# Three attentions whose transposes stand three pairs behind the scores

## The chip, the cores and the metric

The kernel runs on one core of one Trainium2 chip. The time is the device time of one execution in microseconds, and the median of several executions counts. Before the change it is 3695.54 us (three runs, 3688.07 to 3698.82).

## The reference

The input x has 512 tokens of 1024 features. Two blocks follow one another.

The first block has two layers. Each is a gated feed-forward part, a mixer, a second feed-forward part and a gated embedding, all with RMS norms before and after. The mixer joins a stick-breaking attention of 4 heads, a latent attention of 8 heads and a short gated convolution. The latent attention is a causal softmax attention whose queries and keys have 96 features (64 plain and 32 rotated), computed in four blocks of 128 queries:

```python
for start in range(0, S, Q_BLOCK):
    end = start + Q_BLOCK
    sc = (einsum(q_nope[:, start:end], k_nope[:, :end]) + einsum(q_rope[:, start:end], k_rope[:, :end])) * scale
    w = softmax(where(mask, sc, NEG_INF))
    outs.append(einsum(w, v[:, :end]))
```

The second block has two layers, too. The mixer of the first is the DSA attention: 12 query heads share 4 key and value heads, and each query attends to the 128 keys with the highest index score (min(256, 512 / 4)). The mixer of the second is the dilated attention: three patterns of 4 heads each, merged by their log sums. Beside each mixer stands a memory attention: 4 heads, a softmax over 256 memory tokens. Both layers end with a feed-forward part.

## The kernel before

**Layout.** Features lie on the 128 partitions and tokens along the free axis. Each weight is streamed by SyncE in pieces of 128x1024 floats and split by GpSimd into a high and a low part; TensorE multiplies high with high, low with high and high with low. During the attentions no piece is used.

**An attention.** `attend` exists three times, for TensorE (L780), ScalarE (L1142) and VectorE (L1460). The work is cut into rows, a row being one head and one block of 128 queries, and two rows make a pair. In the latent and the DSA attention row block b has b + 1 key blocks (for causality), so four pairs in a row have 1, 2, 3 and 4 key blocks; the latent attention has 16 pairs, the DSA attention 24. In the memory attentions all 8 pairs have 2 key blocks. Each pair goes through these steps:

- TensorE: scores of both rows, and the mask added by a matmul with the identity (L796, L802), into one of two pairs of PSUM banks (psA, psB). It first waits until the exponentials of pair j - 2 are done.
- VectorE: the row maxima, `peak` (L1481).
- ScalarE: the exponentials with their sums, `exponentials` (L1152). They are written to one of four places in the tile PR.
- VectorE: reciprocal and scaling, `normalize` (L1487, L1490).
- TensorE: transposes in groups of up to four 128x128 blocks, `turn_pair` (L813), into one of the two banks of psC. It waits for the normalization and, group by group, until the copy of the group two before has emptied the bank.
- ScalarE: the copy of each group to SBUF, `copy_turned` (L1163).
- TensorE: the products with the values, `weigh` (L827), into psD. It waits for that copy.
- After four pairs: ScalarE copies the output (L1174), and VectorE forms its low part (L1410).

**The order.** Each engine works its own queue in order, and that order is written out by a loop over j. `ahead_of` gives two numbers, `ahead` and `late`. `late` is the distance in pairs between the scores and the transposes. TensorE's loop is

```python
for j in range(len(pairs) + late + 1):
    if j < len(pairs):
        scores(j)
    if 0 <= j - late < len(pairs):
        turn_pair(j - late)
    if j - late - 1 >= 0:
        weigh(j - late - 1)
```

ScalarE's loop (L1166) has in iteration j the exponentials of pair j, then the copies of pair j - late, and when j - late is 4, 8, ... the output copy, which waits for all values up to pair j - late - 1. VectorE's loop (L1492) has in iteration j `peak(j)`, then `normalize(j - 1)`, and when j - late is 4, 8, ... the low part. In the DSA layer's memory attention VectorE also has up to 18 half rounds of the selection, two per iteration (L1466 to L1470), from the first iteration on.

Before the change (ahead, late) is (1, 1) for the dilated attention, which has wide scores and two score places, and (2, 2) for the others: the latent attention (once per layer of the first block), the DSA attention and both memory attentions.

Of the kernel before, what the change touches and what calls it, by code (L numbers as in the profile page):

```python
# [114 lines left out]
def program(nc, A, trips):  # L115
# [209 lines left out]

    def ahead_of(which):

        return (1, 1) if which == "dil" else (2, 2)

    def row_at(which):  # L330

# [193 lines left out]
    def _(pe):  # L525
# [254 lines left out]
        def attend(which):  # L780
            pairs = pairs_of(which)
            ahead, late = ahead_of(which)
            pe.wait_ge(rot_done, n.now(rot_done))
            pe.wait_ge(vt_done, n.now(vt_done))
# [205 lines left out]
    def _(act):  # L990
# [151 lines left out]
        def attend(which):  # L1142
            pairs = pairs_of(which)
            ahead, late = ahead_of(which)
            used_base, turns = n.now(pv_done), 0

# [100 lines left out]
    def _(dve):  # L1247
# [212 lines left out]
        def attend(which, half_rounds=0):  # L1460

            pairs = pairs_of(which)
            ahead, late = ahead_of(which)
            done = 0

# [374 lines left out]
```

## Time and profile before

| | |
|---|---|
| median of three runs | 3695.54 us |
| lowest, highest | 3688.07, 3698.82 us |
| the profiled execution | 3689.66 us |
| its span | 3688.4 us |
| TensorE busy | 3459.0 us (94%) |
| VectorE, ScalarE, GpSimd busy | 1802.9, 719.3, 2418.4 us |
| mean granted clock of TensorE | 0.958 |

The span is the time from the first to the last instruction of the program in the profile. "Granted clock" is the share of TensorE's full clock of 2.4 GHz that the chip gave; it is either 1.0 or 0.5. The chain that ended last is mostly TensorE's matmuls of the feed-forward parts and projections; the attentions are short stretches between them.

### The profile page before, as it was taken

The numbers are of one execution on the slowest core, as the hardware profiler recorded it, in microseconds if no ns is written. First come the engines' busy times: TensorE is split into PE (matmuls) and PEld (weight loads), VectorE is DVE, ScalarE is ACT, GpSimd is POOL, SyncE is SP. The second block draws the span as 40 slices with busy tenths as digits, with TensorE's granted clock in tenths as the row PEclk, the third lists the DMA queues.
The fourth block names the chain that finished last, engine by engine and source line by source line (L and its number), as shares of the span: only waits on it lengthen the run. The fifth ranks groups of instructions, "written<-read, shape, count | busy, mean of one in ns | idle before, by whom it ended". The sixth has DMA issues, their size and how long they took to land. (4 is left out here: it accounts for less than half of the span.)

```text
span 3688.4 us, 42456 instructions
## 1 busy us (share of the span) xinstructions
PE 3459.0 (94%) x15371; PEld 2698.8 (73%) x15384; DVE 1802.9 (49%) x1934; ACT 719.3 (20%) x1404; POOL 2418.4 (66%) x1113
## 2 busy tenths in 40 slices
PE   7999998899998999999899998986999999779998
PEld 6888765688876888775678886654788877558886
DVE  5452535454647545334464474687454323354521
ACT  2110133311123111103321112214311100231100
POOL 7888741488876887763178886650488777328875
PEclk9999998999998999999899999997999999899999
DMA  3233220122331223221022332220122333102232
GB/s 122 97 100 103 86 69 18 58 95 96 109 120 60 94 95 103 86 91 46 18 88 96 104 104 92 92 69 1 56 94 96 103 104 108 40 26 95 97 100 94
DMA packets 84366, 305.98 MB, mean 83 GB/s; under 512 B 9360, under 2 KB 9616, under 8 KB 83856
## 3 DMA queue, kind: packets, MB, share of 16 engines
q1 hardware_dynamic: 80928, 292.59, 23.7%
q10 hardware_dynamic: 3312, 11.71, 0.8%
q8 instruction: 80, 1.31, 0.1%
q14 instruction: 46, 0.38, 0.0%
HBM read 300.07 MB, written 4.19 MB: 82 GB/s over the span
## 5 line engine op out<-in xcount | busy, mean ns | idle before, releaser
L469 POOL TENSOR_TENSOR WH<-raw,zero 128x1024 fp32r<-128x1024 f32 (+1 forms) x554 | 1045.2, 1887 | 1200.6 <-DMA raw<-in_w 1105.7
L471 POOL TENSOR_TENSOR WL<-raw,WH 128x1024 fp32r<-128x1024 f32 (+1 forms) x554 | 1375.0, 2482 | 43.5
L539 PE MATMUL psA<-HH,WH 128*128 128x512 f32 x1216 | 483.6, 398 | 2.3 <-DVE PROJ L1509 2.3
L540 PE MATMUL psA<-HH,WL 128*128 128x512 f32 x1216 | 474.7, 390 | 0.0
L541 PE MATMUL psA<-HL,WH 128*128 128x512 f32 x1216 | 474.7, 390 | 0.0
L541 PE MATMUL psC<-HIDL,WH 128*128 128x512 f32 x1056 | 417.1, 395 | 0.0
L539 PE MATMUL psC<-HIDH,WH 128*128 128x512 f32 x1056 | 417.1, 395 | 0.0
L540 PE MATMUL psC<-HIDH,WL 128*128 128x512 f32 x1056 | 417.1, 395 | 0.0
L1338 DVE TENSOR_TENSOR HIDL<-Y,HIDH 128x512 f32 (+1 forms) x132 | 257.1, 1948 | 126.7 <-ACT HIDH L1060 126.7
L539 PE MATMUL psC<-HH,WH 128*128 128x512 f32 x800 | 314.0, 392 | 3.8 <-DVE HL L1410 3.8
L541 PE MATMUL psC<-HL,WH 128*128 128x512 f32 x800 | 312.3, 390 | 0.0
L540 PE MATMUL psC<-HH,WL 128*128 128x512 f32 x800 | 312.2, 390 | 0.0
L539 PEld LDWEIGHTS psA<-HH,WH 128*128 128x128 f32 x1216 | 229.2, 188 | 60.9 <-issue 10.5
L540 PEld LDWEIGHTS psA<-HH,WL 128*128 128x128 f32 x1216 | 229.0, 188 | 51.3 <-issue 3.9
L541 PEld LDWEIGHTS psA<-HL,WH 128*128 128x128 f32 x1216 | 229.0, 188 | 48.6
L1336 DVE TENSOR_TENSOR Y<-Y 128x512 f32<-128x512 f32 x132 | 253.2, 1918 | 22.1 <-DVE Y L1333 9.6
L539 PE MATMUL psB<-HH,WH 128*128 128x512 f32 x664 | 258.3, 389 | 0.0
L540 PE MATMUL psB<-HH,WL 128*128 128x512 f32 x664 | 258.3, 389 | 0.0
L541 PE MATMUL psB<-HL,WH 128*128 128x512 f32 x664 | 258.3, 389 | 0.0
L1060 ACT ACTIVATE HIDH<-Y 128x512 f32 x132 | 83.5, 633 | 782.4 <-DVE Y L1336 782.4
L541 PEld LDWEIGHTS psC<-HIDL,WH 128*128 128x128 f32 x1056 | 198.2, 188 | 48.3
L540 PEld LDWEIGHTS psC<-HIDH,WL 128*128 128x128 f32 x1056 | 198.2, 188 | 48.2
(274 smaller groups left out, 4896.2 us busy)
## 6 DMA issues: line engine op xcount, KB each, us to landing
raw<-in_w SPq DMA_DIRECT2D x554, 512.0 KB, 3.3
X<-in_x ACTq DMA_DIRECT2D x4, 512.0 KB, 8.9
NRAW<-in_mem ACTq DMA_DIRECT2D x2, 1024.0 KB, 5.2
out<-Y SPq DMA_DIRECT2D x8, 256.0 KB, 2.1
POSI<-in_pos ACTq DMA_DIRECT2D x4, 256.0 KB, 3.0
PRAW<-in_p ACTq DMA_DIRECT2D x2, 512.0 KB, 4.5
table_F<-newF ACTq DMA_DIRECT2D x2, 512.0 KB, 5.1
table_I<-newI ACTq DMA_DIRECT2D x2, 512.0 KB, 7.8
```

The source lines that it names most:

```text
L469: pool.tensor_tensor(WH[j][:, 0:w], raw[j][:, 0:w], zero[:, 0:1].broadcast_to([P, w]), ALU.subtract).then_inc(w_hi, 1)
L471: pool.tensor_tensor(WL[j][:, 0:w], raw[j][:, 0:w], WH[j][:, 0:w], ALU.subtract).then_inc(w_split, 1)
L539: pe.matmul(out, WH[slot][:, w], hi[:, t], start=start and t == 0, stop=False)
L540: pe.matmul(out, WL[slot][:, w], hi[:, t], start=False, stop=False)
L541: mm = pe.matmul(out, WH[slot][:, w], lo[:, t], start=False, stop=stop and t == tiles - 1)
L1060: act.activation(HIDH[:, bass.ds(2 * i + j, 1)].rearrange("p a n -> p (a n)"), US[:, j], ACT.Copy).then_inc(hidh_ready, 1)
L1336: dve.tensor_tensor(US[:, j], US[:, j], GS[:, j], ALU.mult).then_inc(hf_ready, 1)
L1338: dve.tensor_tensor(HIDL[:, at].rearrange("p a n -> p (a n)"), US[:, j], HIDH[:, at].rearrange("p a n -> p (a n)"), ALU.subtract).then_inc ...
```

## The change

One number is changed. For every attention but the dilated one `late` is 3 in place of 2; `ahead` stays 2.

```diff
     def ahead_of(which):
 
-        return (1, 1) if which == "dil" else (2, 2)
+        return (1, 1) if which == "dil" else (2, 3)
```

So in iteration j TensorE issues the scores of pair j, the transposes of pair j - 3 and the values of pair j - 4. ScalarE has the exponentials of pair j and the copies of pair j - 3. The output copy and its low part stand in iterations 7, 11, ... in place of 6, 10, .... The loops run one iteration more.

## Rows read from the trace of the kernel before

**Rows 1.** The page: busy time, share of the span and instructions

```profile
PE 3459.0 (94%) x15371; PEld 2698.8 (73%) x15384; DVE 1802.9 (49%) x1934; ACT 719.3 (20%) x1404; POOL 2418.4 (66%) x1113
```

**Rows 2.** Windows (stretch, length, busy of each engine, clock): latent, memory, DSA

```profile
1762.10:1820.20 58.10, 52.01 (x336) 34.73 (x336) 27.30 (x67) 29.40 (x91) 0.00 (x0) 0.84 0.00 1
2486.30:2530.60 44.30, 24.05 (x128) 14.47 (x128) 37.91 (x111) 13.38 (x42) 0.00 (x0) 0.58 0.00 1
2532.16:2613.96 81.80, 68.84 (x498) 42.90 (x504) 41.07 (x101) 44.29 (x137) 0.00 (x0) 0.86 0.00 1
```

**Rows 3.** Waits (us, times, longest) of the DSA attention, then its memory attention

```profile
PE psC L813 <- DVE PR L1490: 9.2, 6, 2.2
...
PE psC L813 <- DVE PR L1490: 18.5, 8, 4.0
```

**Rows 4.** Timeline (start, us) of TensorE in the DSA attention

```profile
2542.81 0.44 PE L813 MATMUL psC<-cf,PR 128*128 128x128 f32 x2 [0.45 <-ACT PRTb L1163]
...
2543.77 0.70 PE L796 MATMUL psB<-PROJ 64*128 64x256 f32 x4
...
2544.63 1.04 PE L813 MATMUL psC<-cf,PR 128*128 128x128 f32 x8
...
2546.41 0.92 PE L796 MATMUL psA<-PROJ 64*128 64x384 f32 x4
...
2547.59 0.38 PE L813 MATMUL psC<-cf,PR 128*128 128x128 f32 x2
...
2548.93 1.13 PE L796 MATMUL psB<-PROJ 64*128 64x512 f32 x4
...
2550.43 0.60 PE L813 MATMUL psC<-cf,PR 128*128 128x128 f32 x4
...
2551.33 0.49 PE L796 MATMUL psA<-PROJ 64*128 64x128 f32 x4
...
2553.62 0.66 PE L813 MATMUL psC<-cf,PR 128*128 128x128 f32 x4 [1.58 <-DVE PR L1490]
...
2564.77 0.49 PE L796 MATMUL psA<-PROJ 64*128 64x128 f32 x4
```

**Rows 5.** Timeline of ScalarE, same stretch: copy, output copy, first wide exponential, copy

```profile
2549.98 0.38 ACT L1163 ACTIVATE PRTb<-psC 128x256 f32<-128x256 f32 x1
2550.24 0.60 ACT L1174 ACTIVATE OHa<-psD 128x512 fp32r<-128x512 f32 x1
2552.74 0.69 ACT L1152 ACTIVATE PR<-psB,stat 128x512 f32<-128x512 f32 x1 [1.89 <-DVE stat L1481]
...
2554.08 0.59 ACT L1163 ACTIVATE PRTb<-psC 128x512 f32<-128x512 f32 x1
```

**Rows 6.** Timeline of VectorE, same stretch: a peak, the low part, the wide peak

```profile
2544.90 0.69 DVE L1481 TENSOR_REDUCE stat<-psB 128x2 f32<-128x512 f32 x1 [1.51 <-PE psB L802]
...
2550.88 0.69 DVE L1410 TENSOR_TENSOR OLa<-psD,OHa 128x512 fp32r<-128x512 f32 x1 [1.34 <-ACT OHa L1174]
2551.49 1.22 DVE L1481 TENSOR_REDUCE stat<-psB 128x2 f32<-128x1024 f32 x1
```

**Rows 7.** Windows with the granted clock: DSA first, then two cycles of the latent attention

```profile
2551.33:2555.03 3.70, 1.67 (x14) 1.03 (x12) 3.31 (x9) 2.29 (x8) 0.00 (x0) 1.00 0.00 0
2555.03:2558.44 3.41, 3.41 (x20) 2.30 (x19) 0.69 (x2) 1.10 (x4) 0.00 (x0) 0.50 0.01 2
...
1784.16:1787.00 2.84, 1.48 (x12) 1.05 (x10) 2.45 (x7) 1.87 (x6) 0.00 (x0) 1.00 0.00 0
1787.03:1793.86 6.83, 6.74 (x36) 5.21 (x36) 1.91 (x6) 3.44 (x13) 0.00 (x0) 0.50 0.00 0
...
1799.75:1803.10 3.35, 1.88 (x16) 1.28 (x14) 2.96 (x8) 2.39 (x8) 0.00 (x0) 1.00 0.00 0
1803.10:1812.20 9.10, 9.10 (x73) 6.05 (x72) 3.96 (x11) 5.00 (x16) 0.00 (x0) 1.00 0.01 2
```

## The prediction

> **What bounds the kernel now.** I read the page's busy line first: TensorE is busy 94% of the span [rows 1], so a change counts where it takes idle time or slow-clock time from TensorE. Then the stretches of the attentions that the edit reaches [rows 2]: the latent attention (58.1 us, run twice, only the second shown), the DSA attention (81.8 us) and its memory attention (44.3 us); the other memory attention is half as long. Together they are some 260 us, 7% of the span. In the DSA layer's memory attention VectorE is busy 37.9 of 44.3 us; in the DSA and latent ones TensorE is, with a mean clock of 0.86 and 0.84.
>
> Third, the waits of the DSA attention [rows 3]: TensorE's transposes (L813) waited 9.2 us for VectorE's normalization (L1490), six times. Fourth, one cycle of four pairs on each engine [rows 4 to 6]. I name the pairs by their number of key blocks: 1, 2, 3, 4. Before, TensorE issues scores(1), transposes(3), values(2), scores(2), transposes(4), values(3) and so on. After scores(1) it has to transpose pair 3, whose normalization has not come: it idles 1.58 us, issues four blocks, and waits 0.45 us more for ScalarE's copy (L1163), that is for a free transpose bank. Nothing else in the cycle waits. The cycle is 13.44 us (2551.33 to 2564.77).
>
> Fifth, the granted clock. Up to 2555.03 it is 1.00 (2.4 GHz), with TensorE busy 1.67 of 3.70 us; the stretch from there to 2558.44, with TensorE busy throughout, is at 0.50 (1.2 GHz) [rows 7]. That comes back in each of the five later cycles of the DSA attention. A slow stretch costs half its length while TensorE is busy, 1.7 us, so the cycle at full clock would be 11.74 us: 9.5 of work and some 2.2 of waiting, counted from issue to issue (1.66 and 0.6).
>
> **The change part by part.** It adds no instruction and removes none, and no DMA moves. In four places (latent twice, DSA, both memory attentions) the loop runs one iteration more, and per iteration the engines see: TensorE scores(j), transposes(j-3), values(j-4) instead of j-2 and j-3; ScalarE exponentials(j), copies(j-3), and every fourth time the output copy; VectorE peak(j), normalization(j-1) as before, with the low part of the output (L1410) one iteration later. The dilated attention keeps (1, 1).
>
> *The wait that goes.* Transposes now concern a pair normalized an iteration earlier. The 1.66 us and 0.6 us of the old order are gone.
>
> *What is late next.* ScalarE is one in-order queue: the copies of pair j-3 stand behind the exponentials of pair j, and these behind its peak. I walk one cycle of DSA at full clock, with t = 0 at the end of scores(4). Issue times from [rows 4], start to next start: transposes(1)+values(4) 1.34, scores(1) 0.63, transposes(2) 0.53 (with values(1) 0.90), scores(2) 0.86, transposes(4)+values(3) 1.78, scores(3) 1.18, scores(4) 1.50.
> TensorE: transposes(1), values(4) to 1.34; scores(1) to 1.97; transposes(2) to 2.50; now values(1) needs the copy of pair 1.
> VectorE: peak(4) starts 0.27 after the scores (2544.63 to 2544.90, [rows 4, 6]). ScalarE's exponentials start 1.25 after that (2551.49 to 2552.74) and take 1.34 (to 2554.08) [rows 5, 6]: from 1.52 to 2.86. Copy of pair 1 follows, 0.26 to the next start, its data at 3.3. So values(1) waits **0.8 us**, and ends at 3.67. scores(2) to 4.53, first group of transposes(3) to 5.03; the second needs the copy of pair 2.
> ScalarE meanwhile: output copy 3.12 to 3.74, VectorE's low part after it 3.76 to 4.37 (0.61, 2550.88 to 2551.49). Only then VectorE reaches peak(1), which had been ready at 2.2: peak to 4.8 (0.43, by the line through 0.69 at 512 and 1.22 at 1024 elements), exponentials(1) to 5.5 (0.7, a quarter of the width of the 1.34), copy of pair 2 to 6.17 (0.59 and 0.05). So the second group waits **1.14 us**. From there: rest of transposes(3) and values(2) to 7.13 (0.96, 2542.81 to 2543.77), scores(3) 8.31, transposes(4)+values(3) 10.09, scores(4) 11.59. The exponentials that these need (pair 1 at 5.5, pair 2 at 7.4) and the banks are in time.
> The cycle is 11.6 us against 11.74 at full clock: 1.94 us of waiting in place of 2.2. The edit trades one wait for two smaller ones and wins 0.15 us a cycle, 0.6 in four whole cycles. The first cycle has no output copy and by the same walk wins 0.7, the tail 0.3: DSA is 1.6 us shorter at full clock.
> The latent attention has the same order with longer scores: a cycle at full clock is 12.45 us (1799.75 to 1812.20), with 1.47 us of idle time in its first 3.35 [rows 7]. The walk with 1.0 us more of scores gives 12.35, and with first cycle and tail 0.5 us per run, 1.0 for both.
> DSA's memory attention: 18 half rounds of the selection and the peaks keep VectorE busy; after normalization(7) the same transposes, two pairs of values and output copy remain in both orders, so 0. It also has the largest wait for normalization in the profile, 18.5 us [rows 3], but that is VectorE's own pace, and asking later does not shorten it. The other memory attention: TensorE has little idle time in the middle, and its one long wait (about 1.9 us behind the low part) turns into copies that come late: between -1 and +1, taken as 0.
> Sum at full clock: 1.6 + 1.0 = **2.6 us**, of which I'd believe anything from -3 to 8, since a 0.2 us error in the walk counts some 11 times.
>
> *The clock.* The stretches at 0.50 in [rows 7] follow the two waits of 1.58 and 0.45 us, close together. In the new order the waiting is 0.8, then 1.7 us of work, then 1.1: less dense. I count five slow stretches like 2555.03 in DSA, and in the two latent attentions after their start three like 1787.03 (6.83 us) and one half as long: 17.1 + 23.9 = 41 us, costing at most 20. Ends: none of it comes back (0), all comes back (20). In the latent attention one cycle's idle time (1.36 of 2.84 us) was followed by a slow stretch and the same in another cycle (1.47 of 3.35) was not [rows 7]; the 2 us of each DSA cycle always was. The new waits, 1.94 in all with 1.7 of work between them, lie between these two. I take 12 us, about 60%.
> The Trainium skill speaks against this term. Its page TensorE: Matmul & The Clock Gate, section HAM oscillation, has the clock fall when TensorE waits through a long gap between bursts, longer than any wait inside these cycles. Here the trace disagrees: a wait of 1.58 us and one of 0.46 with work between were enough. By the page's main rule the clock would give nothing; its second failure mode, frequent short idling, is nearer to what the rows show.
>
> **Sum.** 2.6 + 12 = 14.6 us. The profiled run took 3689.66 us, 1.3 more than its span of 3688.4; it would take 3675. The median of the three runs is 3695.54, 5.9 above it, and I apply the gain to that: **3681 us**.
>
> **The rivals.**
> *A, the forecast*, 3681, range of its own 3672 to 3689. Chance 0.50.
> *B, the clock stays as it was*: the new waits are still dense enough for a slow stretch per cycle. For it: 1.94 us of waiting is only a tenth less than 2.2, and the page's main rule would give this time too. Against: it is spread wider, and the latent attention was at the edge already. 3695.5 - 2.6 = 3693. Chance 0.27.
> *C, the late copies cost more than the old wait*: place, values(1) and the second group of transposes(3), behind exponentials(4), the output copy and the low part. It decides from the point where the two waits pass 2.2 us in a cycle (1.8 in the latent ones). For it: all three engines now pass through that chain in series, and ScalarE's wide exponentials come before the copy. Price: 0.3 us more in 11 cycles is 3, and if each latent cycle then falls into a slow stretch, which now only three of about eight do, four or five more at 3.1 us make 13: 3711. If the waits only just pass, 3698. Chance 0.13.
> *D, no wait takes its place*: the copies turn out to be no limit, all waiting goes: 2.2 x 5 + 1.8 x 7 is 24 us, and of the clock the 12 again, less what overlaps: 3662. For it: TensorE has 3.5 us of work after scores(4) before it needs the exponentials. Against: the walk shows the copy queued behind them. Chance 0.10.
> That the edit does nothing is excluded by the order of the queues; it could be nothing in time, which is B.
>
> **How the numbers follow.** 0.3% is 11 us, about what a measurement of this kernel can tell from no change. Faster: A but for its upper edge (0.45), D (0.10), little of B (0.02): 0.57. Slower: over half of C, 0.08. Same: 0.35. The range for 8 in 10 leaves out most of D below and the worse half of C above: 3665 to 3698.
>
> **What would show it.** In DSA's waits the rows L813 on L1490 nearly go, and L827 on L1163 (values on copies, 0.8 us each) and L813 on L1163 (1.1 each) take their place. The cycle in DSA at full clock is 11.5 us; the mean clock there goes from 0.86 to 0.90 or more. The DSA memory attention keeps its 44.3 us. Wrong would be: the cycle over 11.8 at full clock (C), the clock still at 0.86 (B), or no wait of values on copies (D).

## The result

The changed kernel takes 3670.39 us (median of five runs, 3668.56 to 3675.29) against 3695.54 before. The ratio of the times is 0.9938, with a 95% interval of 0.9925 to 0.9950: 0.62% or some 23 us faster, clear of the 0.3% that such a measurement can tell from none (the medians alone differ by 25 us). The forecast was 3681 us, faster; the measured time lies inside the range and beyond the likeliest case's own range of 3672 to 3689.

The profiled executions compare as 3689.66 to 3668.56 us, their spans as 3688.4 to 3667.2, 21.2 us less. First the stretches of the attentions in the profile after (columns as in [rows 2]: length, busy time of TensorE's matmuls and weight loads, VectorE, ScalarE, GpSimd, then the clock): the two latent attentions, the DSA layer's memory attention, the DSA attention, and the cycle of four pairs in it.

```profile
610.60:665.03 54.43, 48.84 (x336) 32.55 (x336) 27.09 (x67) 29.57 (x91) 0.00 (x0) 0.89 0.00 1
1754.03:1808.46 54.43, 48.85 (x336) 32.56 (x336) 27.09 (x67) 29.57 (x91) 0.00 (x0) 0.89 0.00 1
2472.34:2516.60 44.26, 26.35 (x128) 15.78 (x128) 37.91 (x111) 13.35 (x42) 0.00 (x0) 0.50 0.00 1
2518.16:2590.31 72.15, 61.36 (x504) 36.98 (x504) 40.67 (x101) 44.55 (x137) 0.00 (x0) 0.96 0.00 1
2536.78:2548.37 11.59, 9.74 (x86) 6.02 (x84) 6.83 (x18) 7.48 (x23) 0.00 (x0) 1.00 0.01 2
```

DSA is 9.7 us shorter (81.8 to 72.15), with the clock at 0.96 in place of 0.86 [rows 2]. The second latent attention is 3.7 us shorter, the first, 59.7 us before, 5.3. Both are now alike to a hundredth. The DSA layer's memory attention kept its 44.3 us, and VectorE's busy time in it (37.91) is the same to the digit. The stretch of the dilated attention with the short memory attention behind it went from 100.4 to 98.5. These add up to 20.6 of the 21.2 us.

A part of the gain is given back at the start of the latent attentions. They begin in a stretch at 0.50, which lasted 8.1 and 7.9 us into them before and 11.9 us in both after. Over all profiles below in which a latent attention begins so, it is 6.9 to 8.5 us in the eight with late 2 and 10.4 to 11.9 us in the fifteen with late 3. TensorE is busy throughout the first of these cycles either way; what makes the stretch longer is not shown.

The waits of the DSA attention after (who waited for whom: us, times, longest), for [rows 3]:

```profile
PE psD L827 <- ACT PRTb L1163: 6.3, 6, 1.4
...
PE psC L813 <- ACT PRTb L1163: 3.9, 4, 1.0
```

The 9.2 us of transposes on VectorE's normalization are gone. In their place the values (L827) wait for ScalarE's copies, six times, and so do second groups of transposes, four times. The timeline of TensorE after, over one cycle, for [rows 4]:

```profile
2535.76 1.09 PE L827 MATMUL psD<-PRTb,VT 128*64 128x128 f32 x16
2536.78 0.49 PE L796 MATMUL psA<-PROJ 64*128 64x128 f32 x4
...
2538.75 0.44 PE L827 MATMUL psD<-PRTb,VT 128*64 128x128 f32 x4 [0.81 <-ACT PRTb L1163]
...
2541.62 0.44 PE L813 MATMUL psC<-cf,PR 128*128 128x128 f32 x2 [1.04 <-ACT PRTb L1163]
...
2548.37 0.49 PE L796 MATMUL psA<-PROJ 64*128 64x128 f32 x4
```

From one scores(1) to the next it is 11.59 us. Before, it was 13.44 with a slow stretch in it. ScalarE and VectorE in the same cycle show why the two waits stand there, for [rows 5] and [rows 6]:

```profile
2536.98 0.69 ACT L1152 ACTIVATE PR<-psB,stat 128x512 f32<-128x512 f32 x1 [1.49 <-DVE stat L1481]
...
2538.32 0.38 ACT L1163 ACTIVATE PRTb<-psC 128x256 f32<-128x256 f32 x1
2538.58 0.60 ACT L1174 ACTIVATE OHa<-psD 128x512 fp32r<-128x512 f32 x1
2540.27 0.37 ACT L1152 ACTIVATE PR<-psA,stat 128x128 f32<-128x128 f32 x1 [1.09 <-DVE stat L1481]
...
2540.97 0.59 ACT L1163 ACTIVATE PRTb<-psC 128x512 f32<-128x512 f32 x1
```

```profile
2539.22 0.69 DVE L1410 TENSOR_TENSOR OLa<-psD,OHa 128x512 fp32r<-128x512 f32 x1 [1.41 <-ACT OHa L1174]
2539.82 0.41 DVE L1481 TENSOR_REDUCE stat<-psA 128x2 f32<-128x256 f32 x1
```

The copy that values(1) need starts at 2538.32, when the wide exponentials are done. The copy that frees the bank for transposes(3) starts at 2540.97: behind exponentials(1), these behind peak(1) at 2539.82, this behind the low part, and that behind the output copy.

### The profile page after: what moved, and what is told of

It reads as the page before. It is cut to its first block and busy times, and to the rows that moved or that the text cites. A ratio compares the mean times of both kernels' runs of the same rounds, so it can differ in the third digit from the quotient of the medians.

```text
span 3667.2 us, 42469 instructions
## 1 busy us (share of the span) xinstructions
PE 3450.9 (94%) x15384; PEld 2691.5 (73%) x15384; DVE 1806.8 (49%) x1934; ACT 719.8 (20%) x1404; POOL 2417.9 (66%) x1113
## 5 line engine op out<-in xcount | busy, mean ns | idle before, releaser
L539 PEld LDWEIGHTS psA<-HH,WH 128*128 128x128 f32 x1216 | 229.7, 189 | 61.2 <-issue 10.4
L539 PEld LDWEIGHTS psC<-HIDH,WH 128*128 128x128 f32 x1056 | 198.2, 188 | 48.1
```

The source lines that it names most:

```text
L539: pe.matmul(out, WH[slot][:, w], hi[:, t], start=start and t == 0, stop=False)
```

## The experiments

Each kernel was timed in runs of its own beside runs of the kernel before. The table has the median, the ratio to the kernel before with its interval, and from the profile the lengths in us of the two latent attentions, of the DSA attention (with the number of separate slow stretches that begin in it), and of the dilated attention with the memory attention behind it; the last column is the rest of the span without the DSA layer's memory attention, which took 45 to 46 us up to the start of the DSA attention in each.

| kernel | median | ratio, interval | latent | DSA (slow) | dilated + memory | outside |
|---|---|---|---|---|---|---|
| before | 3695.5 | 1 | 59.7, 58.1 | 81.8 (5) | 100.4 | 3342 |
| after | 3670.4 | 0.9938, 0.9925 to 0.9950 | 54.4, 54.4 | 72.1 (0) | 98.5 | 3342 |
| x_dsa | 3682.9 | 0.9967, 0.9955 to 0.9978 | 56.4, 60.0 | 71.6 (0) | 100.8 | 3340 |
| x_mla | 3686.2 | 0.9966, 0.9953 to 0.9978 | 54.4, 54.4 | 81.7 (4) | 100.8 | 3350 |
| x_mem | 3693.1 | 0.9985, 0.9974 to 0.9997 | 59.8, 59.9 | 80.2 (4) | 98.6 | 3351 |
| fill | 3673.9 | 0.9938, 0.9924 to 0.9951 | 50.6, 54.0 | 74.6 (0) | 100.8 | 3343 |
| fill3 | 3683.2 | 0.9972, 0.9960 to 0.9984 | 54.4, 57.0 | 75.3 (1) | 98.3 | 3350 |
| dense | 3676.0 | 0.9951, 0.9938 to 0.9965 | 54.4, 54.4 | 77.2 (1) | 98.3 | 3344 |
| dense2 | 3683.9 | 0.9974, 0.9963 to 0.9985 | 56.1, 54.4 | 85.1 (5) | 99.7 | 3342 |
| low_later | 3669.2 | 0.9932, 0.9919 to 0.9945 | 51.5, 52.6 | 69.8 (0) | 98.2 | 3348 |
| copy_first | 3645.9 | 0.9854, 0.9835 to 0.9873 | 50.2, 50.2 | 63.7 (0) | 85.4 | 3354 |
| both | 3642.9 | 0.9857, 0.9842 to 0.9871 | 50.2, 50.2 | 63.9 (0) | 85.4 | 3360 |
| copy_first2 | 3651.9 | 0.9886, 0.9872 to 0.9900 | 47.5, 51.0 | 69.6 (1) | 88.0 | 3343 |
| copy_first_nodil | 3658.9 | 0.9901, 0.9887 to 0.9915 | 46.0, 50.2 | 64.6 (0) | 100.7 | 3359 |

"Outside" moves by up to 19 us though no instruction differs there, so the total of one execution can't tell 5 us; the stages can. The profiled execution is also not the median one: in both it took 3656.4 us against a median of 3642.9, in copy_first2 3646.0 against 3651.9.

### One attention at a time

```diff
-        return (1, 1) if which == "dil" else (2, 3)
+        return (1, 1) if which == "dil" else (2, 3 if which == "dsa" else 2)
```

(x_dsa; x_mla has "mla" in place of "dsa", and x_mem the two memory attentions.)

> Late is 3 in the DSA attention alone, 2 elsewhere. Theory (each attention wins by itself: fewer us of waiting and no slow clock stretches inside it): the DSA attention takes about 72 us in place of 82, the latent ones keep 58 to 60 each, the total falls by about 10 us to 3685. Rival (the slow stretches of one attention depend on where the chip's clock record stood after the part before, so the gain was partly luck of position): the DSA attention keeps some slow stretches of 3.4 us, 74 to 79 us.

> Late is 3 in the two latent attentions alone. Theory: each takes 54.4 us, the DSA attention 82 with its five slow stretches, the total falls by about 9 us plus what lies outside, to 3685. Rival (position): the latent ones differ from each other again by 2 us or more, or the DSA attention changes though its order did not.

> Late is 3 in the two memory attentions alone. Theory (VectorE's selection bounds the one, and the other has little waiting to lose): the first keeps 44.3 us, the second 20 to 22, the total is within 2 us of before apart from noise. Rival (one pair more of distance frees them as well): the first under 43 us, total 5 us or more below.

DSA alone: 71.6 us, no slow stretch begins in it, and the total is 12 us less. The latent ones alone: 54.45 and 54.44 us, and the total is 12 us less by the ratio, 9 by the medians. Where late stayed 2, the slow stretches stayed too: 81.7 us in DSA, 56.4 and 60.0 in the latent ones. So each attention wins by itself. The half of the rival that speaks of position holds for late 2: 56.4 to 60.0 us for the same order of instructions. With late 3 nothing of it was seen in DSA.

These kernels also show a cycle of DSA with late 2 at full clock, which the kernel before does not have with the output copy in it. In x_mla:

```profile
2558.07:2569.98 11.91, 9.72 (x86) 6.07 (x85) 6.93 (x18) 7.38 (x23) 0.00 (x0) 1.00 0.01 1
```

It has the same waits of 1.58 and 0.45 us and takes 11.91 us; in x_mem one takes 11.92. So a slow stretch of 3.41 us costs a cycle 1.5 to 1.6 us (13.44 and 13.49 less 11.91), and the order of late 3 is 0.32 us a cycle shorter at full clock. It also shows that these waits do not always bring the slow clock: of the four pairs of waits of 1.58 and 0.45 us in DSA a slow stretch began within 2 us of the end of the first wait at all four in the kernel before, at two in x_mla and at three in x_mem.

The memory attentions won 1.9 us at the dilated part (98.6), where I had taken 0, between -1 and 1. The short memory attention by itself went from 21.2 to 18.9 us, below the 20 to 22 expected, with one slow stretch beginning in it in place of two. The total of x_mem fell by 5.5 us by the ratio and 1.6 by the medians.

### Is it the clock: extra work for TensorE in the wait

```diff
     def turn_pair(j):
 ...
+                if which in ("mla", "dsa") and len(pairs[j][0][3]) == 3:
+                    pe.wait_ge(pt_done, ...)        # the transpose bank is free
+                    for _ in range(8):
+                        pe.matmul(PC[:, turns % 2, 0:NM], identb[:], mb[:, 0:NM], start=True, stop=True)
                 pe.wait_ge(p_norm, n.full(p_norm, 2))
```

> Kernel before (late 2), but ahead of the wait for the normalization of each three-block pair in the latent and DSA attentions TensorE issues eight matmuls of 384 columns in bf16 into the free transpose bank; their result is overwritten by the transposes. The order and the other engines stay. Theory (most of the change's gain is the clock, and the clock falls because of the waits): at full clock the eight take about 1.3 us of a wait of 1.6, the waits remain in time but the slow stretches inside the attentions go; the DSA cycle is 11.8 to 12 us in place of 13.45, the stage about 74 us, the latent ones 55 to 56, the total falls by 12 to 18 us. Rival (the gain is the waits' own, and the slow stretches merely accompany them): the cycle stays at 13.4 us or grows, total the same or up to 5 us more.

A cycle of DSA in this kernel (late 2), then the whole stage. The timeline of TensorE, with its own line numbers (L813 the extra matmuls, L818 the transposes), then the windows:

```profile
2538.34 0.49 PE L797 MATMUL psA<-PROJ 64*128 64x128 f32 x4
...
2538.89 1.46 PE L813 MATMUL psC<-mb,identb 128*128 128x384 bf16 x8
2540.63 0.66 PE L818 MATMUL psC<-cf,PR 128*128 128x128 f32 x4 [0.28 <-DVE PR L1495]
2541.74 0.44 PE L818 MATMUL psC<-cf,PR 128*128 128x128 f32 x2 [0.45 <-ACT PRTb L1168]
...
2550.25 0.49 PE L797 MATMUL psA<-PROJ 64*128 64x128 f32 x4
```

```profile
2518.75:2593.33 74.58, 69.26 (x546) 41.69 (x552) 41.06 (x101) 44.11 (x137) 0.00 (x0) 0.96 0.00 1
2538.34:2550.25 11.91, 11.02 (x93) 6.77 (x93) 6.93 (x18) 7.38 (x23) 0.00 (x0) 1.00 0.00 1
```

The theory holds, and it gave more than the 12 to 18 us expected: 22 by the medians. The order is that of the kernel before, the normalization comes as late as before, TensorE has eight more matmuls to do in each of 14 pairs (6 in DSA, 4 in each latent attention), which serve nothing, and the kernel is 0.62% faster than before. The cycle is 11.91 us in place of 13.44, at full clock; no slow stretch begins in DSA or in the latent attentions, where nine began before. It is also the 11.91 us of late 2 at full clock without the extra matmuls (x_mla, above), so these cost the cycle nothing and gave it the clock alone. That settles the rival: what the change gave, it gave mostly by the clock. (The first latent attention was at full clock from its start here, which is worth 3.4 us and may not be the experiment's; four other kernels began it so.)

The control puts the same matmuls into the kernel after.

> Kernel after (late 3) with the same eight extra matmuls ahead of each three-block pair's transposes as in fill. Theory (in fill they paid by keeping the clock; here no slow stretch is left to win back): the DSA cycle grows from 11.6 to 11.7 or 12.1 us, of the 1.3 us added some falls into the 1.0 us wait behind it; total 1 to 5 us above the kernel after. Rival (the extra matmuls speed the loop in some other way): total below the kernel after by 3 us or more.

```profile
2551.04:2562.67 11.63, 10.66 (x93) 6.86 (x92) 6.83 (x18) 7.50 (x23) 0.00 (x0) 1.00 0.00 1
```

No gain appeared: the rival is out. In the stages the size was nearly right. The first cycle with an output copy takes 12.45 us (2538.59 to 2551.04), with a late copy (1.34 us) and 0.65 us at the slow clock in it. The three behind it take 11.63 to 11.73, within 0.15 of the kernel after: of the 1.3 us added nearly all falls into the wait for the transpose bank, which is gone there. In the latent attention the cycle is 12.61 us against 12.35. The two latent and the DSA attention together are 5.7 us longer than in the kernel after. But the total rose by some 13 us (0.9972 against 0.9938), more than the 1 to 5 expected, and 8 of them lie outside the attentions, where no instruction differs; what made them is not shown.

### How much waiting brings the slow clock back

```diff
     def copy_turned(j):
 ...
+                if which == "dsa" and pair_blocks(pairs[j]) == 2:
+                    act.activation(T[:, 0], T[:, 1], ACT.Copy)     # dense
+                    act.activation(T[:], T[:], ACT.Copy)           # dense2, in its place
```

(`pair_blocks` counts the blocks of both rows, so this is the pair with one key block; the copies go within a tile whose content is not used.)

> Kernel after (late 3) with one more ScalarE copy of 512 columns ahead of the copy of each one-block pair in the DSA attention; its result is not used. It lengthens the wait of values(1) from 0.8 to 1.3 us. Theory (the clock falls when enough waiting of TensorE comes close together): the cycle at full clock is 12.1 us, and slow stretches come back in some or all of the five later cycles: DSA 75 to 84 us in place of 72, total 3 to 12 us above the kernel after. Rival (late 3 changed the clock by something other than the amount of waiting): no slow stretch inside, DSA 74.5 to 75 us, total 3 us above.

> As dense, with an extra ScalarE copy of 1024 columns in place of 512: the wait of values(1) in the DSA attention becomes about 1.75 us in one piece, the second wait stays 1.04 us, 2.8 us of waiting a cycle, more than before the change (2.0). The cycle at full clock is 12.6 us. Theory (one dense piece of waiting near 2 us brings the slow stretches back): three or more slow stretches inside DSA, its length 80 us or more, total 8 to 15 us above the kernel after. Rival (the second, near wait is what counted before the change, 1.58 and 0.45 us with 0.5 us of work between them; here the two waits stand 1.8 us or more apart): none or one slow stretch, DSA 77 to 79 us, total 5 to 7 us above the kernel after.

TensorE in a cycle of dense, then two windows of it: the whole DSA stage, and a wait in its first cycle:

```profile
2543.52 0.49 PE L796 MATMUL psA<-PROJ 64*128 64x128 f32 x4
...
2546.01 0.44 PE L827 MATMUL psD<-PRTb,VT 128*64 128x128 f32 x4 [1.33 <-ACT PRTb L1165]
...
2548.88 0.44 PE L813 MATMUL psC<-cf,PR 128*128 128x128 f32 x2 [1.04 <-ACT PRTb L1165]
...
2555.63 0.49 PE L796 MATMUL psA<-PROJ 64*128 64x128 f32 x4
```

```profile
2523.67:2600.83 77.16, 62.43 (x498) 38.09 (x504) 40.66 (x101) 47.83 (x143) 0.00 (x0) 0.93 0.00 1
...
2532.64:2535.00 2.36, 0.00 (x2) 0.00 (x1) 1.97 (x8) 2.29 (x7) 0.00 (x0) 1.00 0.00 0
```

The cycle is 12.11 us, as worked out. The waiting in it is 1.33 + 1.04 = 2.37 us, more than the 2.03 before the change, and yet no slow stretch followed any of its four cycles. The one that came, at 2595.49, began 0.9 us behind the wait at the tail of the stage, which is 1.92 us in one piece. So the amount per cycle does not decide. Even the 2.36 us in one piece in the first cycle were followed by full clock; in dense2 a wait of 2.35 us at the same place had a slow stretch right behind it (2532.05).

dense2 has 1.85 us in one piece and 0.95 behind, in a cycle at full clock. The windows show the stage, then the piece with the wait and the one after it:

```profile
2521.44:2606.58 85.14, 69.50 (x498) 42.81 (x504) 40.64 (x101) 50.27 (x143) 0.00 (x0) 0.84 0.00 1
2541.83:2545.70 3.87, 2.11 (x20) 1.29 (x18) 1.47 (x5) 3.15 (x7) 0.00 (x0) 1.00 0.02 4
2545.70:2552.50 6.80, 6.39 (x29) 3.89 (x28) 3.34 (x10) 3.08 (x11) 0.00 (x0) 0.50 0.00 1
```

Five slow stretches are back, two of them twice as long, and the stage takes 85.1 us, 3.3 more than before the change. The theory's numbers held (three or more, 80 us or more, 8 to 15 us in total: 13 by the ratios). A cycle at full clock still exists in it (12.54 us, 2556.61 to 2569.15). Of its four pieces of 1.76 to 1.85 us three had a slow stretch behind them, as nine of the twelve pairs of 1.58 and 0.45 us with late 2 had. Of the four pieces of 1.33 to 1.42 us in dense none had. So a dense piece of waiting near 2 us mostly brings the slow clock, and one of 1.4 us with the next 1.8 us behind it did not. How near the second wait stands counts too, it seems: in the latent attention with late 2 the waits are 1.02 and 0.46 us with 0.7 us between them, less than in dense, and eight of twelve such pairs (before, x_dsa, x_mem) had a slow stretch within 2.5 us. No run varies the gap alone. Why the same waits did it once and not the next time stays open.

### The two waits that are left

```diff
             for j in range(len(pairs) + late + 1):
+                if 0 <= j - late < len(pairs):
+                    copy_turned(j - late)
                 if j < len(pairs):
                     exponentials(j)
-                if 0 <= j - late < len(pairs):
-                    copy_turned(j - late)
```

> Kernel after (late 3), with ScalarE's copies of pair j-3 placed ahead of the exponentials of pair j in its queue. Theory (the two waits left in the cycle, 0.8 us of values(1) and 1.04 us of the second group of transposes(3), come from the copies queued behind the exponentials): both nearly go, the DSA cycle falls from 11.6 to 9.7 us, DSA 62 us, latent 49 to 50 each, total 18 to 22 us below the kernel after, 3650. Rival (the exponentials now wait for transposes(j-3), which stand behind scores(j) on TensorE, and with them the next scores): the cycle falls by less than half a us or grows, total 3665 to 3680.

TensorE over one cycle, and the DSA stage with the stretch of the dilated attention and the memory attention behind it:

```profile
2534.62 0.49 PE L796 MATMUL psA<-PROJ 64*128 64x128 f32 x4
...
2536.32 0.70 PE L796 MATMUL psB<-PROJ 64*128 64x256 f32 x4 [0.17 <-ACT PR L1152]
...
2544.50 0.49 PE L796 MATMUL psA<-PROJ 64*128 64x128 f32 x4
```

```profile
2517.30:2581.01 63.71, 59.29 (x498) 36.82 (x504) 40.58 (x101) 45.10 (x137) 0.00 (x0) 0.97 0.00 1
3151.60:3237.00 85.40, 65.73 (x553) 48.17 (x560) 38.81 (x75) 41.22 (x99) 6.80 (x4) 0.92 0.00 1
```

Both waits are gone: the cycle is 9.88 us (9.7 expected), of which TensorE is busy 9.4. ScalarE does the copies in the time in which it had waited for the peak. That shows that the copies behind the exponentials are the cause of what waits in the kernel after. The edit also reached the dilated attention, which I had not reckoned with: 13 us less there. That made the total 24 us less by the medians, above the 18 to 22 expected; the two latent and the DSA attention alone are 17 us shorter. To part the two:

> Kernel after (late 3) with ScalarE's copies ahead of the exponentials in every attention but the dilated one, which keeps its order. Theory (of the 24 us that copy_first took off the kernel after, the dilated attention had 13): total 10 to 14 us below the kernel after, 3657 to 3660, the dilated part with the short memory attention behind it at 98 us. Rival (the stages shift time to one another through the clock): the total differs from that by over 5 us.

It is 0.9901, 11 to 14 us below the kernel after by median and ratio, as expected in the total. The dilated part is 100.7 us, not the 98 expected.

Moving the low part instead, in the kernel after:

```diff
                 if j < len(pairs):
                     peak(j)
+                for c in due:        # due since the iteration before
+                    low_of(PD[:, c % 2], O_AT[which] + c, which)
 ...
-                    low_of(PD[:, c % 2], O_AT[which] + c, which)
+                    due.append((j - late - 1) // 4)
```

> Kernel after (late 3), with VectorE's low part of the output (L1410) moved behind the next pair's peak instead of ahead of it. Theory (in the cycle the second group of transposes(3) waits because peak(1) stands behind the low part, and exponentials(1) and copy(2) behind that): that wait of 1.04 us goes, the 0.8 us of values(1) stays, the DSA cycle is 10.5 us in place of 11.6, total 9 to 12 us below the kernel after. Rival (the wait is ScalarE's own, since copy(2) is behind two exponentials and the output copy in any case): the cycle falls by 0.3 us or less.

The wait at the second group of transposes(3) vanished, as the theory has it. The cycle became 11.04 us, not 10.5, because another wait came up (TensorE in this kernel; the first row is the wait that was to stay):

```profile
2544.52 0.44 PE L827 MATMUL psD<-PRTb,VT 128*64 128x128 f32 x4 [0.82 <-ACT PRTb L1163]
...
2548.95 1.06 PE L813 MATMUL psC<-cf,PR 128*128 128x128 f32 x8 [0.46 <-ACT PRTb L1163]
```

The low part now holds up normalization(4) and peak(2), and with them the copies of pair 3. The stages are 7 us shorter, the total 1 to 2: 6 us more lie outside. It is a miss on the total, for which 9 to 12 us were expected.

> Copies ahead of the exponentials and the low part behind the next peak, both on the kernel after. Theory (with the copies first, TensorE's own issue time bounds the cycle at 9.5 us, and peak(1) has slack): equal to copy_first within 2 us. Rival (with the copies first the low part is what still holds the exponentials): 5 to 10 us below copy_first.

The stages equal copy_first's to 0.2 us, the totals are alike in their intervals.

> Kernel before (late 2) with the copies ahead of the exponentials in all attentions, the dilated one included, as in copy_first. Theory (with late 2 the wait for the normalization stays whatever ScalarE's order is, only the 0.45 us behind it goes): DSA cycle at full clock 11.2 us, some slow stretches stay, DSA 72 to 78 us, latent 54 to 57, the dilated part 13 us shorter as in copy_first; total 3665 to 3675, 20 us or more above copy_first. Rival (ScalarE's order alone was the fault, and late 2 would do as well): total within 5 us of copy_first.

With late 2 the cycle is 10.96 us (11.2 expected), 1.1 more than with late 3, and DSA 69.6 us against 63.7: late 3 is worth 6 us there on top of the better order.

```profile
2529.60 0.87 PE L813 MATMUL psC<-cf,PR 128*128 128x128 f32 x6 [1.30 <-DVE PR L1490]
```

The wait for the normalization stays, but it is 1.30 us and the only one of the cycle, and none of the four such waits had a slow stretch behind it; the one that came stands behind a wait of 1.95 us at the tail. I had counted too many slow stretches. The total is 6 us above copy_first by the medians (12 by the ratios), not 20, and the attentions in the table, 6.7 us longer together, account for the 6. It also means that this edit with late 2 beats the change under study: 0.9886 against 0.9938, and without the dilated attention's share the latent and DSA attentions are still shorter than in the kernel after (47.5, 51.0 and 69.6 us; the first was at full clock from its start).

## Why the prediction was right

*The wait that goes* was right: no transposes of DSA wait for the normalization any more.

*What is late next* was right in place and size: values(1) were to wait 0.8 us and did so for 0.81, the second group of transposes(3) 1.14 and did for 1.04, and the cycle was to be 11.6 us and is 11.59, in the latent attention 12.35 and is 12.35. The walk over three queues, with durations from rows, is all it took. (One of its steps, 5.5 + 0.59 + 0.05, is 6.14 and not 6.17.) Copy_first removed its cause and with it both waits.

*The stages at full clock.* The cycle before at full clock was put at 11.74 us, with half of the slow stretch, 1.7 us, taken off. It is 11.91 (x_mla), and the issue times of the prediction's own walk say so too: they add up to 9.65 us of work, not 9.5, and with 2.26 of waiting to 11.91. So a slow stretch costs less and the order itself gives more than forecast: 0.32 us a cycle and not 0.15. By that, the five slow stretches of DSA cost 7.8 us and 1.9 of its 9.7 us are the order's own, against 1.6 forecast. The first memory attention won 0, as said, the other with the dilated attention 1.9 instead of 0.

*The clock* is the term that was mis-sized. I took 12 of at most 20 us, a choice between two ends and no result of the walk, in the belief that some slow stretches would stay. None did. That the split waits would free clock was reasoned; that the forecast of 14.6 us in all came within its range of the 23 to 25 measured owes something to how wide the range was. In the latent attentions the three stretches of 6.83 us had cost 3.2 us each (15.63 us with one against 12.47 without in x_dsa) and the short one some 1.5, 11.0 in all; the longer slow start took back about 3.6. That leaves 7.4 of their 9.0 us to the clock and 1.6 to the order. With the 7.8 of DSA the clock gave 15.2 us by this estimate. The sum is then 15.2 + 3.5 + 1.9 = 20.6 us, against 21.1 between the profiled executions and 25.1 between the medians. The rest is scatter outside the attentions as far as can be told: the total of the kernel before alone ranged over 10.8 us.

*The rivals.* B, the clock as it was, is refuted by the 0.96 of DSA. With a wait of 1.85 us in one piece the slow stretches came back (dense2), so it was near. C did not happen: the two waits are 1.85 us together, under the 2.2. Dense, with 2.37 us, is slower at full clock as C has it (12.11 us against 11.91), but the slow clock that C adds did not come with it: an amount per cycle was the wrong measure for that. D, no new wait, is what copy_first reaches by another edit.

The Trainium skill's page TensorE: Matmul & The Clock Gate has, in the section HAM oscillation, a long idle gap as the cause of the slow clock. Here the trace disagrees: waits of 1.58 and 0.45 us sufficed in nine of twelve cycles of DSA, and filling the first removed the slow stretches. The section A second HAM failure mode, which tells of frequent short idling between groups of matmuls, fits this kernel's rows.

## What to carry to other kernels

When one software-pipelined loop runs over several in-order queues, walk one cycle of it per engine with measured durations before moving anything: the distance between two steps only helps until the next queue order binds, and here the place of the copies in ScalarE's queue was worth about as much again as the distance (17 us in the latent and DSA attentions, against 19). Where TensorE's clock shows slow stretches behind waits, reckon a wait at its own length plus a little under half of the slow stretch behind it (1.5 us of 3.41 here); in this kernel breaking 2 us of dense waiting into two pieces of 0.8 and 1.0, 1.8 us apart, was worth more than the waiting saved. And judge such an edit by the length of its own stages, since the rest of a 3.7 ms kernel scatters by more.

## What was not expected of the hardware

Useless matmuls made the kernel 0.62% faster: eight of 384 columns, 1.46 us, stood in each of 14 waits, and no slow stretch began in the three attentions, where nine had begun before; the cycle of DSA is as long with them as without them at full clock, 11.91 us. And the same instructions of the latent attention took 56.4 to 60.0 us with late 2, but 54.43 to 54.45 us in seven of the eight latent attentions that ran with late 3 and nothing else changed in them (after, x_mla, dense, dense2; the eighth took 56.05): with the waits broken up, nearly all of the scatter of the stage went as well.
